# Sixteen of 22 k-pairs in seven products, VectorE's weight sum one quadruple ahead, and a later load for a lone plain quadruple

## The chip, the cores and the metric

The kernel runs on one core of one Trainium2 chip. The metric is the device time of one execution in microseconds (us).

## What is computed

One layer of a hybrid encoder on 256 tokens of width 2048, all in float32. First a mixer (sliding-window attention beside a gated linear recurrence), then the feed-forward block, in which the change lies:

```python
u = h @ w_up                      # 2048 -> 2 * 5632
u = causal depthwise conv of 3 taps(u)
a, b = split(u)
x = x + (silu(a) * b) @ w_down    # 5632 -> 2048
```

## The kernel before, in words

**Products in three parts.** TensorE takes each float32 product as three matmuls: high part by high part, high by low, low by high. A weight block comes from HBM by a DMA that SyncE's queue (SP) issues; ScalarE (ACT) writes its rounded high part (hi); VectorE (DVE) writes the rest, weight minus high part, as its low part (lo); then TensorE may use it. The text calls three such matmuls of 128x128 by 128x512 a **set**.

**The last product**, gated activations by w_down, is the down stage. Its 44 row tiles of w_down make 22 k-pairs. It runs twice, for two pairs of 512 output columns (pair 0 and pair 1), so there are 44 **quadruples** (four 128x512 blocks of w_down and four token-by-column outputs), numbered q = 22 * pair + place here. A quadruple is done in one of two ways. A plain one ("four", lines around 2190) takes 8 sets: two pieces a and b, 4 sets each. A **seven** (function `seven`) is Winograd's form of the 2x2 block product: 7 sets in pieces a (2 sets), b (3) and c (2), with sums of weights and sums of activations. PATTERNS (line 82) writes the kind of each place: S is a seven; C, D, c and d are plain ones. C and D differ in which blocks of the high-part buffer they use; c and d lie in a large slot.

**Where the sums come from.** Two of a seven's weight blocks are sums of neighbours that GpSimd (POOL) forms ahead of time in HBM (u_sums, function `column_block` and the loop behind it): per k-pair two copying DMAs of 512 KB and two accumulating ones, paced by TensorE's progress in steps of SUM_STEP units. The other two sums are VectorE's: t2 = t1 + b21 (line 1694) and t4 = t2 + b22 (line 1696), which fill piece c. They read piece b as loaded. The sums of activations are made by VectorE and ScalarE in the up stage (`sums_of_activations`, `hi_of_sums`), one group each, for the first SEVENS groups; 14 of them stay in SBUF (RESIDENT_SUMS), the others are parked in DRAM (`park_sums`) and fetched back by `fetch_sums` into memory that the x2 tile later takes over. `fetch_x2` brings back the residual in four parts, at the places in X2_BACK_AT.

**Buffers.** From q = 4 on, raw weights and their low parts have three large slots (`slots`), which sevens and c take in turn, and a small one (slot3a, slot3b) for C and D. High parts have two slots, by q modulo 2. So the load of a seven's piece a is issued when the same piece of the seven three turns earlier has been used (`wait_for_slot`, through units_used), and ScalarE's high part of a piece waits until the piece of q - 2 in the same blocks has been used (`hi_piece_before`).

**Order of the work.** Each engine's order is written out. SP: for each q, `load_seven` (four DMAs: line 638, 256 KB, and 639, 256 KB of u_sums, for piece a; line 641, 512 KB, and 643, 256 KB of u_sums, for piece b) or `load_four` (line 650, two DMAs of 512 KB). ScalarE: `hi_of`, the pieces in turn (line 1131); piece c waits for t4. VectorE: `lo_of` (line 1703), which for a seven is: low part of a, t2, t4, low part of b, low part of c (line 1680). At q = 22 and 43 VectorE also merges the Winograd sums of a pair into the output (`free_the_banks`, `rest_of_merge`, `add_last`). TensorE waits with units_split for a piece's low part.

```python
PATTERNS = ["CCCCSSSSSDSSSSSDSSSSSc", "CcSSDSSSSSDSSSSSDSSSCc"]
SUM_STEP = (13, 3)
X2_BACK_AT = [[5, 5, 17, 17], [13, 13, 19, 19]]
```

Of the kernel before, what the change touches and what calls it, by code (L numbers as in the profile page):

```python
# [35 lines left out]
ALU = mybir.AluOpType  # L36
# [42 lines left out]
Q_DOWN = Q_UP + 2 * UP_GROUPS  # L79
QUADRUPLES = KT_FF // 2  # L80
COLUMN_PAIRS = OUT_GROUPS // 2
PATTERNS = ["CCCCSSSSSDSSSSSDSSSSSc", "CcSSDSSSSSDSSSSSDSSSCc"]
KINDS = "".join(PATTERNS)
SEVENS = PATTERNS[0].count("S")
SEVEN_AT = [[at for at, kind in enumerate(pattern) if kind == "S"] for pattern in PATTERNS]
EIGHT_AT = [[at for at, kind in enumerate(pattern) if kind != "S"] for pattern in PATTERNS]
RESIDENT_SUMS = 14
# [8 lines left out]
OLD_RING = 4  # L96
SLOTS = 4
SMALL_SLOT = SLOTS - 1


def slots_in_turn():

    slot_of, turn = [None] * OLD_RING, 0
    for kind in KINDS[OLD_RING:]:
        if kind in "CD":
            slot_of.append(SMALL_SLOT)
        else:
            slot_of.append(turn % SMALL_SLOT)
            turn += 1
    return slot_of  # L110


SLOT_OF = slots_in_turn()
HI_SLOTS = 2
SUM_STEP = (13, 3)
SCRATCH = 1024

G_OUT = 0
# [10 lines left out]
def hybrid_layer(nc, x, attn_norm, w_in, q_norm, k_norm, sinks, lb_logits, hg_norm, w_out,  # L129
                 ffn_norm, w_up, conv_w, conv_b, w_down, out):  # L130
    ctx = ExitStack()
    with ctx:
# [3 lines left out]
        def sem(name):  # L136
            return ctx.enter_context(nc.semaphore(name))
# [223 lines left out]
        down_loaded = {piece: [sem(f"down_loaded_{piece}{n}") for n in range(SLOTS)] for piece in "ab"}  # L361
        four_loaded = {piece: [sem(f"four_loaded_{piece}{n}") for n in range(SMALL_SLOT)] for piece in "ab"}
        t2_made, t4_made = sem("t2_made"), sem("t4_made")
# [52 lines left out]
        def q_of(pair, at):  # L416
            return pair * QUADRUPLES + at

        def is_seven(pair, at):
            return PATTERNS[pair][at] == "S"  # L420

        def seven_of(pair, at):

            return pair * SEVENS + SEVEN_AT[pair].index(at)

        def pieces_of(q):
            return "abc" if is_seven(*divmod(q, QUADRUPLES)) else "ab"

        def piece_number(q, piece):

            return Q_DOWN * RING + sum(len(pieces_of(n)) for n in range(q)) + "abc".index(piece)
# [11 lines left out]
        def raw_piece_before(q, piece):  # L443
            return last_piece_in(q, piece, lambda m: SLOT_OF[m] == SLOT_OF[q], raw_blocks_of)
# [14 lines left out]
        def raw_blocks_of(q, piece):  # L459

            if SLOT_OF[q] == SMALL_SLOT:
                return {"a": slice(0, 2), "b": slice(2, 4)}[piece]
            return blocks_of(q, piece)

        def slot_of(q, piece, as_lo):

            if SLOT_OF[q] == SMALL_SLOT:
                return slot3["ab".index(piece)][as_lo][:, :, :]
            return slots[SLOT_OF[q]][as_lo][:, blocks_of(q, piece), :]

        def raw_of(q, piece):
            return slot_of(q, piece, 0)

        def lo_slot(q, piece):
            return slot_of(q, piece, 1)

        def hi_slot(q, piece):
            return hi_slots[q % HI_SLOTS][:, blocks_of(q, piece), :]
# [4 lines left out]
        def loaded_of(q, piece):  # L483
            return (four_loaded if in_large_slot(q) else down_loaded)[piece][SLOT_OF[q]]

        def down_loads(q):

            n = sum(is_seven(*divmod(m, QUADRUPLES)) + 1 for m in range(OLD_RING, q + 1)
                    if SLOT_OF[m] == SLOT_OF[q] and in_large_slot(m) == in_large_slot(q))
            return 16 * n  # L490

        def wait_for_down(engine, q, piece):
            engine.wait_ge(loaded_of(q, piece), down_loads(q))

        def wait_until_used(engine, number):
            engine.wait_ge(units_used, number + 1 + RING)
# [22 lines left out]
        def out_both(pair):  # L519
            return slice(2 * pair * GT, 2 * (pair + 1) * GT)  # L520
# [1 line left out]
        X2_PARTS = [(1, 1), (1, 0), (0, 0), (0, 1)]  # L522
        X2_PARTS_APART = 2 - (PARKED_SUMS - 1)
        SUMS_BACK_AT = [5, 7]
        X2_BACK_AT = [[5, 5, 17, 17], [13, 13, 19, 19]]
        FIRST_HALF, SECOND_HALF = slice(0, GT // 2), slice(GT // 2, GT)

        def last_half(pair):
# [14 lines left out]
        def _(sp):  # L543
# [16 lines left out]
            for i in range(2):  # L560
                c = slice(i * HEAD_DIM, (i + 1) * HEAD_DIM)
# [44 lines left out]
            def fetch_x2(pair, part):  # L606

                if part == 0 and pair == 0:
                    sp.wait_ge(x2_parked, 16 * OUT_GROUPS)
                t, b = X2_PARTS[part]  # L610
                if part == X2_PARTS_APART:
                    wait_until_used(sp, piece_number(q_of(pair, SEVEN_AT[pair][LAST_PARKED_TURN]), "c"))
                sp.dma_start(x2[:, t, b * GT:(b + 1) * GT], parked_v[:, t, out_columns(pair, b)]).then_inc(x2_back, 16)
# [9 lines left out]
            def wait_for_slot(q, piece):  # L623

                before = raw_piece_before(q, piece)
                if before is not None:
                    wait_until_used(sp, before)
                elif SLOT_OF[q] == 2:
                    wait_until_used(sp, LAST_OLD - 3 if piece == "a" else LAST_OLD - 1)
                elif SLOT_OF[q] == SMALL_SLOT and piece == "b":  # L630
                    wait_until_used(sp, LAST_OLD)
# [13 lines left out]
            def load_four(pair, at):  # L645

                q = q_of(pair, at)
                for r, piece in enumerate("ab"):
                    wait_for_slot(q, piece)
                    sp.dma_start(raw_of(q, piece).rearrange("p b m -> p (b m)"),  # L650
                                 w_down_v[:, 2 * K_PAIR_AT[pair][at] + r, out_both(pair)])\
                        .then_inc(loaded_of(q, piece), 16)
# [5 lines left out]
            for pair in range(COLUMN_PAIRS):  # L658
                for at in range(QUADRUPLES):
# [8 lines left out]
                    for part in range(len(X2_PARTS)):  # L668
                        if at == X2_BACK_AT[pair][part]:
                            fetch_x2(pair, part)  # L670
# [3 lines left out]
        def _(pool):  # L674
# [52 lines left out]
            def wait_for_step(step):  # L727
                pool.wait_ge(units_used, (Q_F0 + 3) * RING + step * SUM_STEP[0] // SUM_STEP[1] + RING)

# [428 lines left out]
        def _(dve):  # L1158
# [63 lines left out]
            for b in (2, 3):  # L1222
                last = dve.memset(bank[b][:, KEYS:], 0.0)
# [3 lines left out]
            for h in range(2):  # L1227
                s = slice(h * HEAD_DIM, (h + 1) * HEAD_DIM)
# [448 lines left out]
            def split(q, piece):  # L1677

                dve.wait_ge(units_hi, piece_number(q, piece) + 1)
                dve.tensor_tensor(lo_slot(q, piece), raw_of(q, piece), hi_slot(q, piece).bitcast(F32),  # L1680
                                  ALU.subtract).then_inc(units_split, 1)

            def sums_of_weights(pair, at):

                q, s = q_of(pair, at), seven_of(pair, at)
                b21, b22, t1 = [raw_of(q, "b")[:, m, :] for m in range(3)]
                t2, t4 = [raw_of(q, "c")[:, m, :] for m in range(2)]
                wait_for_down(dve, q, "b")
                before = raw_piece_before(q, "c")
                if before is not None:  # L1690
                    wait_until_used(dve, before)
                elif SLOT_OF[q] == 2:
                    wait_until_used(dve, LAST_OLD)
                dve.tensor_tensor(t2, t1, b21, ALU.add).then_inc(t2_made, 1)
                dve.wait_ge(t2_made, s + 1)
                dve.tensor_tensor(t4, t2, b22, ALU.add).then_inc(t4_made, 1)  # L1696

            def lo_of(pair, at):

                q = q_of(pair, at)  # L1700
                for piece in pieces_of(q):
                    if piece == "b" and is_seven(pair, at):
                        sums_of_weights(pair, at)
                        dve.wait_ge(t4_made, seven_of(pair, at) + 1)
                    split(q, piece)
                    if (q, piece) == ADDED_BEHIND:
                        add_last(0)
                    if (q, piece) in MERGE_BEHIND:
                        free_the_banks(MERGE_BEHIND.index((q, piece)))
# [12 lines left out]
            for pair in range(COLUMN_PAIRS):  # L1722
                for at in range(QUADRUPLES):
                    if q_of(pair, at) >= OLD_RING:
                        lo_of(pair, at)
                    for merging in range(COLUMN_PAIRS):
                        if q_of(pair, at) == MERGE_BEHIND[merging][0]:
                            rest_of_merge(merging)
# [541 lines left out]
```

## Time and profile before

| what | us |
|---|---|
| median of 3 runs (1083.17 to 1083.44) | 1083.18 |
| the profiled execution | 1083.67 |
| its span in the trace | 1081.9 |
| TensorE busy | 1076.5 (100% of the span) |
| VectorE busy | 908.9 (84%) |
| ScalarE busy | 631.5 (58%) |
| down stage on TensorE, first weight load to last matmul | 859.02 to 1078.34 |

The profiled execution took 1.8 us more than its span, which counts from the first to the last recorded instruction. The granted TensorE clock is full in all slices.

### The profile page before, as it was taken

The numbers are of one execution on the slowest core, as the hardware profiler recorded it, in microseconds if no ns is written. First come the engines' busy times: TensorE is split into PE (matmuls) and PEld (weight loads), VectorE is DVE, ScalarE is ACT, GpSimd is POOL, SyncE is SP. The second block draws the span as 40 slices with busy tenths as digits, with TensorE's granted clock in tenths as the row PEclk, the third lists the DMA queues.
The fourth block names the chain that finished last, engine by engine and source line by source line (L and its number), as shares of the span: only waits on it lengthen the run. The fifth ranks groups of instructions, "written<-read, shape, count | busy, mean of one in ns | idle before, by whom it ended". The sixth has DMA issues, their size and how long they took to land.

```text
span 1081.9 us, 18172 instructions
## 1 busy us (share of the span) xinstructions
PE 1076.5 (100%) x6549; PEld 930.6 (86%) x6549; DVE 908.9 (84%) x1371; ACT 631.5 (58%) x925; POOL 72.0 (7%) x100
## 2 busy tenths in 40 slices
PE   9999999999999999999999999999999999999998
PEld 8888888888888888888888888888898888888887
DVE  6877988889656578888888888887877899999997
ACT  6677666757544655545555555545555566656663
POOL 4500000000000000000000000000000000000000
PEclk9999999999999999999999999999999999999999
DMA  7645677777788968788787878888887877887782
GB/s 262 195 139 154 194 203 228 193 243 203 225 234 259 258 216 245 222 237 218 247 228 233 237 208 256 229 232 239 245 233 223 236 260 263 282 279 254 287 313 95
DMA packets 185070, 249.08 MB, mean 230 GB/s; under 512 B 9125, under 2 KB 143158, under 8 KB 184758
## 3 DMA queue, kind: packets, MB, share of 16 engines
q1 hardware_dynamic: 170118, 212.30, 60.6%
q0 software_dynamic: 12480, 31.46, 15.2%
q10 hardware_dynamic: 2416, 4.60, 1.2%
q8 instruction: 31, 0.51, 0.2%
q14 instruction: 25, 0.20, 0.1%
HBM read 243.75 MB, written 36.04 MB: 259 GB/s over the span
## 4 chain that ended last, share of the span: by engine, by line
PE 98%; DMA 1%; DVE 1%; ACT 0%; issue 0%; SPq 0%; DVEq 0%; ACTq 0%
PE bank L1769 38%; PE bank L1777 20%; PE bank L2154 7%; PE bank L2153 7%; PE bank L2152 7%; PE bank L2005 3%; PE bank L1837 3%; PE bank L1839 3%; PE bank L1838 3%; PE bank L2006 3%; PE bank L2007 3%; PE bank L1739 1%; DMA xt<-in_x_dram 1%; PE bank L2044 0%; PE bank L1924 0%; PE bank L1814 0%
## 5 line engine op out<-in xcount | busy, mean ns | idle before, releaser
L758 ACT CAST w_hi<-raw 128x1024 fp32r<-128x1024 f32 x299 | 313.1, 1051 | 254.8 <-PE bank L1777 122.7
L1161 DVE TENSOR_TENSOR w_lo<-raw,w_hi 128x1024 fp32r<-128x1024 f32 x299 | 363.9, 1222 | 107.7 <-ACT w_hi L758 107.2
L1769 PE MATMUL bank<-hs,w_hi 128*128 128x512 f32 x1792 | 423.0, 391 | 0.0
L1769 PEld LDWEIGHTS bank<-hs,w_hi 128*128 128x128 f32 x1792 | 331.2, 188 | 66.3 <-issue 0.9
L1777 PEld LDWEIGHTS bank<-hs,w_lo 128*128 128x128 f32 x1792 | 224.6, 191 | 5.7 <-issue 0.2
L1777 PE MATMUL bank<-hs,w_lo 128*128 128x256 f32 x1792 | 227.3, 283 | 0.0
L1131 ACT CAST hi_slot<-slot 128x1024 fp32r<-128x1024 f32 (+1 forms) x96 | 110.9, 1188 | 68.5 <-DVE slot L1696 37.3
L1680 DVE TENSOR_TENSOR slot_lo<-slot,hi_slot 128x1024 fp32r<-128x1024 f32 (+1 forms) x96 | 128.7, 1387 | 4.5 <-ACT hi_slot L1131 3.6
L2154 PE MATMUL bank<-hi_slot,gated 128*128 128x512 f32 (+1 forms) x202 | 78.2, 387 | 0.0
L2152 PE MATMUL bank<-hi_slot,gated 128*128 128x512 f32 (+1 forms) x202 | 78.2, 387 | 0.0
L1598 DVE SCALAR_TENSOR_TENSOR C<-U,cols,C 128x256 f32<-128x256 f32 x176 | 73.4, 479 | 0.0
L2153 PE MATMUL bank<-slot_lo,gated 128*128 128x512 f32 (+1 forms) x146 | 56.4, 386 | 0.0
L1062 ACT ACTIVATE C<-U,cols 128x256 f32<-128x256 f32 x88 | 48.2, 596 | 12.1 <-DVE U L1172 12.1
L743 POOL DMA_DIRECT2D u_sums<-in_w_ffn_down_dram x30 | 27.4, 914 | 344.6 <-PE bank L1769 143.7
L1837 PE MATMUL bank<-w_hi,mix 128*128 128x512 f32 x128 | 50.3, 393 | 0.0
L2005 PE MATMUL bank<-w_hi,hs 128*128 128x512 f32 x128 | 50.3, 393 | 0.0
L1839 PE MATMUL bank<-w_hi,mix 128*128 128x512 f32 x128 | 49.9, 390 | 0.0
L2007 PE MATMUL bank<-w_hi,hs 128*128 128x512 f32 x128 | 49.8, 389 | 0.0
L1838 PE MATMUL bank<-w_lo,mix 128*128 128x512 f32 x128 | 49.8, 389 | 0.0
L2006 PE MATMUL bank<-w_lo,hs 128*128 128x512 f32 x128 | 49.8, 389 | 0.0
L2152 PEld LDWEIGHTS bank<-hi_slot,gated 128*128 128x128 f32 x202 | 37.9, 188 | 7.8
L2154 PEld LDWEIGHTS bank<-hi_slot,gated 128*128 128x128 f32 x202 | 37.9, 188 | 7.6
(249 smaller groups left out, 1197.8 us busy)
## 6 DMA issues: line engine op xcount, KB each, us to landing
raw<-in_w_ffn_up_dram SPq DMA_DIRECT2D x176, 512.0 KB, 4.8
u_sums<-in_w_ffn_down_dram POOLq DMA_DIRECT2D x60, 512.0 KB, 6.7
raw<-in_w_in_dram SPq DMA_DIRECT2D x52, 512.0 KB, 4.6
slot<-in_w_ffn_down_dram SPq DMA_DIRECT2D x36, 512.0 KB, 4.8
raw<-in_w_in_dram SPq DMA_DIRECT2D x64, 256.0 KB, 3.3
raw<-in_w_out_dram SPq DMA_DIRECT2D x32, 512.0 KB, 5.1
slot<-u_sums SPq DMA_DIRECT2D x60, 256.0 KB, 5.6
slot<-in_w_ffn_down_dram SPq DMA_DIRECT2D x30, 256.0 KB, 4.1
```

Of the source, the lines that this page charges most:

```text
L758: act.copy(w_hi[:, i, :], raw[:, i, :]).then_inc(units_hi, 1)
L1131: act.copy(hi_slot(q, piece), raw_of(q, piece)).then_inc(units_hi, 1)
L1161: dve.tensor_tensor(w_lo[:, i, :], raw[:, i, :], w_hi[:, i, :].bitcast(F32), ALU.subtract)\
L1680: dve.tensor_tensor(lo_slot(q, piece), raw_of(q, piece), hi_slot(q, piece).bitcast(F32), ALU.subtract).then_inc(units_split, 1)
L1769: m = pe.matmul(banks[b][:, :], w_hi[:, i, c], hs[:, 4 * i + k, :], start=(first and k == 0), stop=(final and k == 3))
L1777: m = pe.matmul(banks[b][:, 0:SEQ], w_lo[:, i, c], hs[:, 4 * i + k, 0:SEQ], start=False, stop=False)
L1837: pe.matmul(banks[t][:, :], x_hi, hi, start=(k0 + k == 0), stop=False)
L1839: last = pe.matmul(banks[t][:, :], x_lo, hi, start=False, stop=(k0 + k == k_all - 1))
L2005: pe.matmul(o, x_hi, hi, start=(u == 0 and k == 0), stop=False)
L2152: pe.matmul(dst[:, :], x_hi, hi, start=start, stop=False)
L2153: pe.matmul(dst[:, :], x_hi, lo, start=False, stop=False)
L2154: return pe.matmul(dst[:, :], x_lo, hi, start=False, stop=stop)
```

## The change

The patterns get one more S per pair (16 instead of 15) and one plain quadruple fewer: q = 9 becomes a seven, D stands at q = 11 alone in pair 0, and nine sevens follow each other from 12 to 20; in pair 1, D stands at 26, 34 and 42, with seven sevens between (27 to 33, 35 to 41). With that SEVENS is 16 and two sums of activations are parked instead of one. POOL's steps are 4 units apart instead of 13/3. The load of every quadruple in the small slot waits until piece b of the quadruple before it has landed. VectorE forms t2 of q + 1 in front of the last low part of q, and t4 behind it, for all sevens from q = 9 on. Three of the four parts of x2 come back at 14 and 15.

```diff
--- before.py
+++ after.py
@@ -79,7 +79,7 @@
 Q_DOWN = Q_UP + 2 * UP_GROUPS
 QUADRUPLES = KT_FF // 2
 COLUMN_PAIRS = OUT_GROUPS // 2
-PATTERNS = ["CCCCSSSSSDSSSSSDSSSSSc", "CcSSDSSSSSDSSSSSDSSSCc"]
+PATTERNS = ["CCCCSSSSSSSDSSSSSSSSSc", "CcSSDSSSSSSSDSSSSSSSDc"]
 KINDS = "".join(PATTERNS)
 SEVENS = PATTERNS[0].count("S")
 SEVEN_AT = [[at for at, kind in enumerate(pattern) if kind == "S"] for pattern in PATTERNS]
@@ -96,6 +96,7 @@
 OLD_RING = 4
 SLOTS = 4
 SMALL_SLOT = SLOTS - 1
+SUMMED_AHEAD = [q for q, kind in enumerate(KINDS) if kind == "S" and q > OLD_RING + 4]
 
 
 def slots_in_turn():
@@ -112,7 +113,7 @@
 
 SLOT_OF = slots_in_turn()
 HI_SLOTS = 2
-SUM_STEP = (13, 3)
+SUM_STEP = (4, 1)
 SCRATCH = 1024
 
 G_OUT = 0
@@ -522,7 +523,7 @@
         X2_PARTS = [(1, 1), (1, 0), (0, 0), (0, 1)]
         X2_PARTS_APART = 2 - (PARKED_SUMS - 1)
         SUMS_BACK_AT = [5, 7]
-        X2_BACK_AT = [[5, 5, 17, 17], [13, 13, 19, 19]]
+        X2_BACK_AT = [[5, 14, 14, 14], [7, 15, 15, 15]]
         FIRST_HALF, SECOND_HALF = slice(0, GT // 2), slice(GT // 2, GT)
 
         def last_half(pair):
@@ -645,6 +646,8 @@
             def load_four(pair, at):
 
                 q = q_of(pair, at)
+                if SLOT_OF[q] == SMALL_SLOT:
+                    wait_for_down(sp, q - 1, "b")
                 for r, piece in enumerate("ab"):
                     wait_for_slot(q, piece)
                     sp.dma_start(raw_of(q, piece).rearrange("p b m -> p (b m)"),
@@ -1680,29 +1683,38 @@
                 dve.tensor_tensor(lo_slot(q, piece), raw_of(q, piece), hi_slot(q, piece).bitcast(F32),
                                   ALU.subtract).then_inc(units_split, 1)
 
-            def sums_of_weights(pair, at):
-
-                q, s = q_of(pair, at), seven_of(pair, at)
-                b21, b22, t1 = [raw_of(q, "b")[:, m, :] for m in range(3)]
-                t2, t4 = [raw_of(q, "c")[:, m, :] for m in range(2)]
+            def first_sum_of_weights(q):
+
+                b21, _, t1 = [raw_of(q, "b")[:, m, :] for m in range(3)]
                 wait_for_down(dve, q, "b")
                 before = raw_piece_before(q, "c")
                 if before is not None:
                     wait_until_used(dve, before)
                 elif SLOT_OF[q] == 2:
                     wait_until_used(dve, LAST_OLD)
-                dve.tensor_tensor(t2, t1, b21, ALU.add).then_inc(t2_made, 1)
-                dve.wait_ge(t2_made, s + 1)
-                dve.tensor_tensor(t4, t2, b22, ALU.add).then_inc(t4_made, 1)
-
-            def lo_of(pair, at):
-
-                q = q_of(pair, at)
+                dve.tensor_tensor(raw_of(q, "c")[:, 0, :], t1, b21, ALU.add).then_inc(t2_made, 1)
+
+            def second_sum_of_weights(q):
+
+                t2, t4 = [raw_of(q, "c")[:, m, :] for m in range(2)]
+                dve.wait_ge(t2_made, seven_of(*divmod(q, QUADRUPLES)) + 1)
+                dve.tensor_tensor(t4, t2, raw_of(q, "b")[:, 1, :], ALU.add).then_inc(t4_made, 1)
+
+            def lo_of(q):
+
+                here, after = KINDS[q] == "S", q + 1 in SUMMED_AHEAD
                 for piece in pieces_of(q):
-                    if piece == "b" and is_seven(pair, at):
-                        sums_of_weights(pair, at)
-                        dve.wait_ge(t4_made, seven_of(pair, at) + 1)
+                    last = piece == pieces_of(q)[-1]
+                    if last and after:
+                        first_sum_of_weights(q + 1)
+                    if here and piece == "b":
+                        if q not in SUMMED_AHEAD:
+                            first_sum_of_weights(q)
+                            second_sum_of_weights(q)
+                        dve.wait_ge(t4_made, seven_of(*divmod(q, QUADRUPLES)) + 1)
                     split(q, piece)
+                    if last and after:
+                        second_sum_of_weights(q + 1)
                     if (q, piece) == ADDED_BEHIND:
                         add_last(0)
                     if (q, piece) in MERGE_BEHIND:
@@ -1722,7 +1734,7 @@
             for pair in range(COLUMN_PAIRS):
                 for at in range(QUADRUPLES):
                     if q_of(pair, at) >= OLD_RING:
-                        lo_of(pair, at)
+                        lo_of(q_of(pair, at))
                     for merging in range(COLUMN_PAIRS):
                         if q_of(pair, at) == MERGE_BEHIND[merging][0]:
                             rest_of_merge(merging)
```

## Rows read from the trace of the kernel before

**Rows 1.** The page's chain that ended last, by engine.
```profile
PE 98%; DMA 1%; DVE 1%; ACT 0%; issue 0%; SPq 0%; DVEq 0%; ACTq 0%
```

**Rows 2.** Whom TensorE waited for: total us, times, longest; the longest wait.
```profile
PE bank L1744 <- DVE all_mean L1221: 1.1, 1, 1.1
```

**Rows 3.** Busy time by stretch: PE, PEld, DVE, ACT, POOL, clock, DMA share, GB/s.
```profile
1009.00:1019.00 10.00, 10.00 (x46) 8.29 (x45) 9.91 (x10) 6.89 (x6) 0.00 (x0) 1.00 0.99 354
760.00:859.00 99.00, 99.00 (x573) 87.75 (x572) 78.64 (x107) 50.84 (x63) 6.01 (x8) 1.00 0.83 234
```

**Rows 4.** TensorE's timeline, start and duration: two weight loads, the last matmul.
```profile
859.02 0.19 PEld L2152 LDWEIGHTS bank<-w_hi,gated 128*128 128x128 f32 x1
...
859.70 0.19 PEld L2152 LDWEIGHTS bank<-w_hi,gated 128*128 128x128 f32 x1
...
1078.34 0.28 PE L2154 MATMUL bank<-hi_slot,gated 128*128 128x256 f32 x1
```

**Rows 5.** VectorE's timeline around the plain quadruple 9 and the seven 10.
```profile
897.64 2.90 DVE L1680 TENSOR_TENSOR slot_lo<-slot,hi_slot 128x1536 fp32r<-128x1536 f32 x2
900.45 1.22 DVE L1680 TENSOR_TENSOR slot3a_lo<-slot3a,hi_slot 128x1024 fp32r<-128x1024 f32 x1
...
902.75 1.22 DVE L1680 TENSOR_TENSOR slot_lo<-slot,hi_slot 128x1024 fp32r<-128x1024 f32 x1
903.89 0.69 DVE L1694 TENSOR_TENSOR slot<-slot 128x512 f32<-128x512 f32 x1
904.61 0.69 DVE L1696 TENSOR_TENSOR slot<-slot 128x512 f32<-128x512 f32 x1
905.34 4.03 DVE L1680 TENSOR_TENSOR slot_lo<-slot,hi_slot 128x1536 fp32r<-128x1536 f32 x3
909.28 0.68 DVE L1694 TENSOR_TENSOR slot<-slot 128x512 f32<-128x512 f32 x1
```

**Rows 6.** VectorE's timeline in the merge of q = 22.
```profile
963.58 0.69 DVE L1662 TENSOR_TENSOR x<-x,bank 128x512 f32<-128x512 f32 x1
964.18 0.68 DVE L1663 TENSOR_TENSOR x<-x,bank 128x512 f32<-128x512 f32 x1
...
966.70 1.22 DVE L1680 TENSOR_TENSOR slot3b_lo<-slot3b,hi_slot 128x1024 fp32r<-128x1024 f32 x1
```

**Rows 7.** SyncE's queue: issue time and duration of DMAs.
```profile
899.25 0.43 SPq L643 DMA_DIRECT2D slot<-u_sums  x1
...
911.80 0.33 SPq L638 DMA_DIRECT2D slot<-in_w_ffn_down_dram  x1
...
919.44 0.43 SPq L650 DMA_DIRECT2D slot3a<-in_w_ffn_down_dram  x1
...
953.96 0.33 SPq L650 DMA_DIRECT2D slot<-in_w_ffn_down_dram  x1
```

**Rows 8.** DMAs issued at 899.25, 911.80, 953.96, 954.33, 955.32, 1035.34: size, us to landing.
```profile
slot<-u_sums SPq DMA_DIRECT2D x1, 256.0 KB, 5.3
slot<-in_w_ffn_down_dram SPq DMA_DIRECT2D x1, 256.0 KB, 3.3
slot<-in_w_ffn_down_dram SPq DMA_DIRECT2D x1, 512.0 KB, 4.7
slot3a<-in_w_ffn_down_dram SPq DMA_DIRECT2D x1, 512.0 KB, 6.4
slot<-in_w_ffn_down_dram SPq DMA_DIRECT2D x1, 512.0 KB, 8.8
slot<-u_sums SPq DMA_DIRECT2D x1, 256.0 KB, 9.1
```

**Rows 9.** VectorE's timeline at the seven 14, behind whose load stood a plain one.
```profile
926.44 0.69 DVE L1694 TENSOR_TENSOR slot<-slot 128x512 f32<-128x512 f32 x1 [0.89 <-DMA slot<-u_sums]
...
928.02 1.76 DVE L1680 TENSOR_TENSOR slot_lo<-slot,hi_slot 128x1536 fp32r<-128x1536 f32 x1 [0.17 <-ACT hi_slot L1131]
```

**Rows 10.** The DMA view of 900 to 960: GB/s in 40 slices of 1.5 us.
```profile
GB/s 376 380 332 229 315 130 0 0 67 229 217 307 220 307 325 335 195 365 417 391 381 376 404 376 391 117 11 0 168 209 287 302 232 280 333 232 107 257 393 243
```

**Rows 11.** The up stage, 400 to 859: one of VectorE's sums of activations.
```profile
L1635 DVE TENSOR_TENSOR C<-C 128x128 f32<-128x128 f32 x15 | 4.4, 292 | 0.5
```

## The prediction

> **What bounds the kernel now.** I read the chain of waits first: TensorE holds 98% of it [rows 1]. The waits by engine come next: the longest wait of TensorE in the whole execution is 1.1 us, at its start [rows 2]. So the kernel is as long as TensorE's instructions, and whatever shortens them helps until another engine falls behind. The busy time by stretch shows which one is near: in the down stage VectorE is busy 9.91 of 10 us, in the up stage 78.6 of 99 [rows 3]. The timelines then give each price.
>
> TensorE: a set takes 859.70 - 859.02 = 0.68 us [rows 4]. Counting from 859.02, 320 full sets of 0.680 and the last four of half width (0.36 each) end at 1078.2, and the last matmul starts at 1078.34 [rows 4]: no stall in the stage. A seven is 7 x 0.68 = 4.76 us, a plain quadruple 8 x 0.68 = 5.44.
>
> VectorE: from t2 of one seven to t2 of the next is 909.28 - 903.89 = 5.39 us, of which t2 and t4 are 905.34 - 903.89 = 1.45 and the three low parts 3.94 [rows 5]. A plain quadruple is 902.75 - 900.45 = 2.30. So VectorE loses 0.63 us on each seven and gains 3.14 on each plain one. It lives on its lead, which the plain quadruples refill. At q = 14 its low part of b ends at 928.02 + 1.76 = 929.78 [rows 9]; TensorE comes there 105 sets after 859.02, at 930.46. That lead is 0.7 us.
>
> **The change, part by part.**
>
> *One more seven per pair.* Two sets less: -1.36 us of TensorE, on the path. VectorE gets a seven for a plain one, twice.
>
> *t2 ahead.* t4 needs t2, so today it starts 0.72 behind it [rows 5]. Two sums that don't need each other start 0.60 apart [rows 6]. With a low part between them I price each at 0.60: a seven is 3.94 + 1.20 = 5.14 us, and its loss is 0.38. This holds for the 27 sevens from q = 9 on: 27 x 0.25 = 6.8 us less. Two exchanged quadruples add 2 x (5.14 - 2.30) = 5.7. In sum VectorE has 1.1 us less to do and TensorE 1.36 less, so the balance of the stage is as before. What counts is the order. The Trainium skill ("VectorE: DVE Perf Modes", "The DRAIN you can't avoid") says that chained operations take the same time with or without a semaphore between them; by it the new order saves nothing and a seven stays at 5.39. The rows speak against it: 0.72 with the wait, 0.60 without.
>
> *The new run 4 to 10.* VectorE is at the low part of c of q = 8 at 897.64 + 1.67 = 899.31 [rows 5]. Now t2 of 9 stands ahead of it. The b of 10 is loaded at 899.25 + 5.3 = 904.55 [rows 7, 8]; that of 9 is one seven earlier, at 899.8. From there, with 0.60 for a sum, 1.14 and 1.67 for low parts: t2 899.8, c 900.4, t4 901.5, a 902.1, b 903.3; then t2 of 10 904.95, c 905.55, t4 906.7, a 907.3, b 908.4 to 910.2, c to 911.3. TensorE needs b of 10 at 910.7 and c at 912.8. The thinnest lead is 0.5. No stall, taken at 0; half a microsecond more lateness would show.
>
> *The later load.* TensorE reaches q = 11 (D) at 859.02 + 81 x 0.68 = 914.13 and q = 12 at 919.57. SP now waits for b of 10, until 904.6. D's two loads follow at 904.6 and 905.1, and right behind them, since their slot has been free from 903.2 (65 sets), those of q = 12: 905.6, 906.0, 906.4, 906.8. The last one brings the sum block that t2 of 12 needs. So 2.36 MB are asked for within 2.2 us, and q = 13 adds its own from 907.2. D itself lands in time: the first two of such a burst took 4.7 and 6.4 us [rows 8], 909.3 to 911.5, and TensorE wants it at 914.1.
>
> When does b of 12 land? Call it x. The nearest case is the burst at 953.96, four loads of 512 KB (2.10 MB) in 1.4 us: the last landed at 955.32 + 8.8 = 964.1, 10.15 behind the first issue [rows 7, 8]. From 904.65 that gives 914.8; the 0.26 MB more, at the 354 GB/s of [rows 3], give 915.5. I take the middle, x = 915.2. Lower end: the fastest first landing, 3.3 [rows 8], and 2.1 MB behind it at 417 GB/s, the best slice of [rows 10], give 912.9. Upper end: 906.85 + 9.1, the slowest landing of such a block [rows 8], 916.0.
>
> What x costs: VectorE does t2 at x, low b of 11 (ends x + 1.82), t4, a of 12, b of 12 (ends x + 5.23). With 0.1 for the signal, TensorE waits at b of 11 (due 916.85) from x = 914.9 on, and comes to b of 12 with a lead of 915.6 - x, or 0.7 once it has itself waited. Eight sevens follow in pair 0, 8 x 0.38 = 3.0 us of loss: the stall is x - 912.6. In pair 1, D at 34 meets the same order with six sevens behind b of 35, 2.3 us of loss: the stall is the same x less 913.3 (in pair 0's time). At 915.2 that is 2.6 + 1.9 = 4.5; at the ends 0.3 and 6.1. At q = 26 the wait costs nothing, since the small slot is still in use then. At q = 22 it puts the loads some 4 us later, behind which come the merge and its 12 sums; the lead there was 971.3 (165 sets) less 966.70 + 1.22 [rows 6], 3.4 us, and TensorE is late by then itself: 0, at most 1.5.
>
> *The rest, at zero.* Four more GpSimd DMAs before the down stage (64 for 60) in 252 units instead of 256, off every chain; the last is issued earlier than now. Six more operations of VectorE on one up group, about 2 us at 0.29 and more apiece [rows 11], beside 20 idle of 99 [rows 3]; ScalarE's two copies and the second parked block likewise. Fetching 0.39 MB more of parked sums lies at q = 5 and 29, and the three x2 parts at 14 and 15, where nothing is due for some 8 us. Without these covers they would cost up to 1 us each.
>
> **Sum.** -1.36 + 4.5 = +3.1. The profiled execution took 1083.67 (its span and 1.8 around it), 0.5 above the median of the runs; it would become 1086.8. Against the median of 1083.18 that is **1086.3 us**.
>
> **The rivals.**
> *In time after all (not slower).* If the burst is moved at the lower end's rate, x is 912.9, the lead of 2.7 at b of 12 lasts over nearly all nine sevens, and the result is 1083.18 - 1.36 + 0.3 = 1082.1. It decides at the landing of b of 12: each 0.1 us earlier than 915.2 gives back 0.2. For it: the total of bytes is small against 10 us, and D's load no longer stands beside b of 10, the thing that made VectorE wait 0.89 us at q = 14 [rows 9]. Against it: the burst at 953.96. [...]
> *Half.* x between 913.5 and 914.7: stalls of 1 to 3.5 us, about 1083.5.
> *The new order saves nothing.* A seven stays at 5.39: losses of 0.63 over eight and six sevens, 4.4 and 3.1, and 1.3 more at q = 9, 10, 27 to 33 and 11: 1083.18 - 1.36 + 8.8 = 1090.6.
> *The merge at q = 22 is late too:* 1.5 more, 1087.7.
> *Something not seen* makes it faster by more than 1.36 us, which the products removed can't.
>
> **How the numbers follow.** About 0.2% (2.2 us) is what a measurement of this kernel can tell from no change. Forecast 0.47; in time 0.26; half 0.16; merge late too 0.05; order saves nothing 0.04; not seen 0.02. Slower: 0.47 + 0.05 + 0.04 = 0.56. Same: 0.26 + 0.16 = 0.42, since 1082.1 is only 0.1% below. Faster: 0.02. The range holds in time, half and the forecast with its upper end (1083.18 - 1.36 + 6.1 = 1087.9): 1081.8 to 1088.0. The forecast's own is 1085.4 to 1088.0.
>
> **What would show it.** TensorE's waits must show low parts of pieces (line 1680) for q = 11 or 12, 16 to 20 and 38 to 41, in all 4 to 5 us; VectorE idle some 3 us ahead of t2 of 12 and of 35, released by a DMA of u_sums; those blocks landing 8 us or more behind their issue. A seven on VectorE at 5.14 us shows the order right. If TensorE has no wait in the stage and the last matmul starts 1.4 us earlier, the late load was wrong; a pitch of 5.39 means the order was.

## The result, and the profile after

The changed kernel takes **1085.65 us** (median of 13 runs, 1085.0 to 1086.63), the kernel before beside it 1083.09 (13 runs, 1082.94 to 1083.44). The ratio is 1.0023, with a 95% interval of 1.0016 to 1.0031: slower by 2.6 us. Predicted were 1086.3 and a range of 1081.8 to 1088.0. The profiled execution took 1085.14, its span 1083.4.

The chain of waits is TensorE's as before [rows 1], and TensorE's longest wait is still the 1.1 us at its start [rows 2]:

```profile
PE 99%; DVE 1%; ACT 0%; issue 0%; DVEq 0%; ACTq 0%
```

The down stage tells the difference. TensorE's timeline, with its first and last weight load of the stage (the last of before stood at 1078.22):

```profile
858.25 0.19 PEld L2164 LDWEIGHTS bank<-w_hi,gated 128*128 128x128 f32 x1
...
1079.73 0.19 PEld L2166 LDWEIGHTS bank<-hi_slot,gated 128*128 128x128 f32 x1
```

From first to last that is 221.48 us; before, 1078.22 - 859.02 = 219.20, without a stall. Two sets fewer would make it 217.84. So **the stage has 3.64 us of stalls** and is 2.28 longer. Below, the stall of any kernel with 16 sevens is its length less 217.84, and of one with 15 less 219.20. (That the stage starts 0.77 us earlier comes from the start-up and not from the change: six small weight loads there took 0.74 us in this profile and 1.34 in that of before, and in a run below whose kernel differs from before only by SyncE's wait in the down stage they took 0.74 too, and the stage starts at 858.43.)

The waits by engine between 859 and 1082 name who holds TensorE up (columns: total us, times, longest):

```profile
ACT hi_slot L1134 <- DVE slot L1701: 40.1, 27, 2.0
...
DVE slot L1695 <- DMA slot<-u_sums: 7.0, 4, 2.3
PEld bank L2164 <- DVE slot_lo L1683: 6.3, 21, 0.4
...
DVE slot_lo L1683 <- ACT hi_slot L1134: 0.7, 2, 0.4
```

TensorE waits 21 times for a low part. The 6.3 us are more than the stall of 3.64, because each wait as shown has some 0.13 us in it that TensorE doesn't lose: a small gap stands ahead of any weight load, and the load behind a wait follows sooner than usual. VectorE, in turn, waited four times for the block that its sum t2 reads, 7.0 us in all. ScalarE's 40 us are its waits for t4, and they reach nobody: VectorE waited for a high part of a seven only 0.7 us. VectorE's timeline has the four, and between them seven after seven without a gap:

```profile
899.23 0.69 DVE L1695 TENSOR_TENSOR slot<-slot 128x512 f32<-128x512 f32 x1 [1.06 <-DMA slot<-u_sums]
...
913.51 0.69 DVE L1695 TENSOR_TENSOR slot<-slot 128x512 f32<-128x512 f32 x1 [1.62 <-DMA slot<-u_sums]
...
918.66 0.69 DVE L1695 TENSOR_TENSOR slot<-slot 128x512 f32<-128x512 f32 x1
919.26 1.22 DVE L1683 TENSOR_TENSOR slot_lo<-slot,hi_slot 128x1024 fp32r<-128x1024 f32 x1
920.39 0.69 DVE L1701 TENSOR_TENSOR slot<-slot 128x512 f32<-128x512 f32 x1
921.00 2.89 DVE L1683 TENSOR_TENSOR slot_lo<-slot,hi_slot 128x1024 fp32r<-128x1024 f32 x2
923.80 0.69 DVE L1695 TENSOR_TENSOR slot<-slot 128x512 f32<-128x512 f32 x1
...
1004.31 0.69 DVE L1695 TENSOR_TENSOR slot<-slot 128x512 f32<-128x512 f32 x1 [2.30 <-DMA slot<-u_sums]
...
1029.27 0.69 DVE L1695 TENSOR_TENSOR slot<-slot 128x512 f32<-128x512 f32 x1 [2.02 <-DMA slot<-u_sums]
```

The idle times belong to t2 of q = 9, 12, 30 and 35. From 918.66 to 923.80 is 5.14 us, a seven in the new order (5.39 in the old [rows 5]).

SyncE's queue shows the burst that the new wait makes: D's two loads, then the four of q = 12. The landings under it are those of the loads issued at 903.69, 904.06 and 906.29:

```profile
903.69 0.33 SPq L653 DMA_DIRECT2D slot3a<-in_w_ffn_down_dram  x1
904.06 0.43 SPq L653 DMA_DIRECT2D slot3b<-in_w_ffn_down_dram  x1
904.54 0.43 SPq L639 DMA_DIRECT2D slot<-in_w_ffn_down_dram  x1
905.01 0.52 SPq L640 DMA_DIRECT2D slot<-u_sums  x1
905.58 0.67 SPq L642 DMA_DIRECT2D slot<-in_w_ffn_down_dram  x1
906.29 0.65 SPq L644 DMA_DIRECT2D slot<-u_sums  x1
```

```profile
slot3a<-in_w_ffn_down_dram SPq DMA_DIRECT2D x1, 512.0 KB, 4.1
...
slot3b<-in_w_ffn_down_dram SPq DMA_DIRECT2D x1, 512.0 KB, 6.2
...
slot<-u_sums SPq DMA_DIRECT2D x1, 256.0 KB, 7.2
```

906.29 + 7.2 = 913.5, which is where t2 of 12 starts. The busy time by stretch (columns as in [rows 3]) shows it from the other side: around the burst VectorE is not full and the DMAs move 402 GB/s; in the stalls at 939 it is full to the last hundredth; 1019 holds the wait for b of 35.

```profile
909.00:919.00 10.00, 10.00 (x46) 8.27 (x45) 8.38 (x9) 6.62 (x6) 0.00 (x0) 1.00 1.04 402
939.00:949.00 10.00, 9.99 (x43) 7.51 (x42) 10.00 (x11) 6.47 (x7) 0.00 (x0) 1.00 0.77 267
...
1019.00:1029.00 10.00, 9.98 (x44) 7.69 (x43) 8.25 (x8) 5.51 (x6) 0.00 (x0) 1.00 0.86 263
```

Note that a stalled TensorE still reads 9.99 of 10 busy; only the starts of its weight loads, and their number (x42 against x45), tell.

**Two theories.** The wait at q = 30 (1004.31) is the longest of the four, and no load of a plain quadruple is near it: the last block of b of 30 was issued at 998.79 and landed 5.5 us later, which is what such a block takes in a steady run (5.3 in [rows 8]). The prediction has no such wait. So there are two explanations to weigh:

- *A, the burst*: SyncE's wait bunches D's loads with the next seven's, so b of 12 and b of 35 are late.
- *B, the cap*: t2 of q + 1 now stands in front of q's last low part, so b of q + 1 is wanted some 2.0 us earlier than in the old order: 5.14 us ahead of the end of its low part, where it was 1.45 + 1.67 = 3.12. But its load can't be issued earlier: it waits until b of three turns before has been used. Once VectorE has a good lead, it runs into that landing and idles; the lead is cut, at q = 30 to about 0.75 us: low b of 30 ends at 1009.46, and TensorE comes to it 221 sets and 1.7 us of stall behind 858.25, at 1010.2.

### The profile page after: what moved, and what is told of

It is laid out like the page before. It is cut to its first block, busy times and chain, and to the rows that moved or that the text cites. A ratio compares the mean times of both kernels' runs of the same rounds, so it can differ in the third digit from the quotient of the medians.

```text
span 1083.4 us, 18159 instructions
## 1 busy us (share of the span) xinstructions
PE 1078.1 (100%) x6543; PEld 927.1 (86%) x6543; DVE 911.1 (84%) x1383; ACT 632.5 (58%) x929; POOL 75.1 (7%) x104
## 4 chain that ended last, share of the span: by engine, by line
PE 99%; DVE 1%; ACT 0%; issue 0%; DVEq 0%; ACTq 0%
PE bank L1781 38%; PE bank L1789 20%; PE bank L2164 7%; PE bank L2165 7%; PE bank L2166 7%; PE bank L2017 3%; PE bank L1849 3%; PE bank L2019 3%; PE bank L1850 3%; PE bank L1851 3%; PE bank L2018 3%; PE bank L1751 1%; PE bank L1756 1%; PE bank L2056 0%; PE bank L1936 0%; PE bank L1826 0%
## 5 line engine op out<-in xcount | busy, mean ns | idle before, releaser
L1134 ACT CAST hi_slot<-slot 128x1024 fp32r<-128x1024 f32 (+1 forms) x102 | 116.4, 1186 | 67.1 <-DVE slot L1701 40.1
L1683 DVE TENSOR_TENSOR slot_lo<-slot,hi_slot 128x1024 fp32r<-128x1024 f32 (+1 forms) x102 | 138.1, 1387 | 0.9 <-ACT hi_slot L1134 0.7
L2164 PE MATMUL bank<-hi_slot,gated 128*128 128x512 f32 (+1 forms) x194 | 75.5, 389 | 0.0
L2166 PE MATMUL bank<-hi_slot,gated 128*128 128x512 f32 (+1 forms) x194 | 75.1, 387 | 0.0
L2165 PE MATMUL bank<-slot_lo,gated 128*128 128x512 f32 (+1 forms) x154 | 59.6, 387 | 0.0
L2164 PEld LDWEIGHTS bank<-hi_slot,gated 128*128 128x128 f32 x194 | 36.4, 188 | 9.1 <-DVE slot_lo L1683 1.7
L2166 PEld LDWEIGHTS bank<-hi_slot,gated 128*128 128x128 f32 x194 | 36.4, 188 | 7.6
```

The lines of the kernel that those rows point to most:

```text
L1134: act.copy(hi_slot(q, piece), raw_of(q, piece)).then_inc(units_hi, 1)
L2164: pe.matmul(dst[:, :], x_hi, hi, start=start, stop=False)
L2165: pe.matmul(dst[:, :], x_hi, lo, start=False, stop=False)
L2166: return pe.matmul(dst[:, :], x_lo, hi, start=False, stop=stop)
```

## The experiments

"Stall" is as defined above, from the profiled execution. Ratios are against the kernel before, timed beside each run.

### One part of the change undone: the late load

The wait is taken out; everything else is as after.

```diff
-                if SLOT_OF[q] == SMALL_SLOT:
-                    wait_for_down(sp, q - 1, "b")
```

> The changed kernel without SyncE's wait ahead of the small slot's loads. Theory A (the burst: the wait makes D's loads and those of the next seven one burst, and b of 12 and of 35 land late): most of the 3.7 us of TensorE's waits goes, about 1 us is left, 1083.0 us, and VectorE's idle time ahead of t2 of 12 and 35 falls from 1.6 and 2.0 us to under 0.8. Theory B (the cap: with t2 formed one piece earlier, a load that is issued when b of the seven three turns before is used comes too late for any lead over 0.7 us, whoever waits in SyncE): 2.2 to 3.2 us of waits stay, in the last sevens of each run, 1083.9 to 1084.9 us.

Measured: 1084.37 us (11 runs, 1083.49 to 1084.76), ratio 1.0009 (1.0000 to 1.0019); stage 220.64, stall 2.80. This is theory B's range; A's 1083.0 is out. The wait is worth 0.8 us by the stage and 1.3 by the medians, no more. VectorE's timeline shows what is left (its waits of over 1 us):

```profile
906.02 0.69 DVE L1693 TENSOR_TENSOR slot<-slot 128x512 f32<-128x512 f32 x1 [1.34 <-DMA slot<-u_sums]
...
1005.06 0.69 DVE L1693 TENSOR_TENSOR slot<-slot 128x512 f32<-128x512 f32 x1 [2.57 <-DMA slot<-u_sums]
```

The second is the wait at q = 30 again, without any burst. The first is t2 of 10: D's loads are back beside b of 10. The wait had moved that lateness from 10 to 12, not only made one. So 1.1 of the 2.8 us, at q = 9 and 10, come from D's loads together with the early t2, and 1.7 from the last sevens of the runs.

### One part undone: the sum's place

```diff
-SUMMED_AHEAD = [q for q, kind in enumerate(KINDS) if kind == "S" and q > OLD_RING + 4]
+SUMMED_AHEAD = []
```

> The changed kernel with both weight sums behind the seven's own piece a, as before (a seven takes VectorE 5.39 us instead of 5.14). Theory A: the late burst stays and each seven loses 0.63 instead of 0.38: the waits grow to 5 to 6 us, 1087.0 us. Theory B: the cap on the lead rises from 0.7 to 2.7 us and pays for the slower sevens: 2 to 3 us of waits, 1083.7 to 1084.7 us.

Measured: 1087.23 us (5 runs, 1085.52 to 1087.46), ratio 1.0035 (1.0021 to 1.0049); stage 223.06, stall 5.22. Here A is right and B wrong: with 16 sevens and the late load, the old order is 1.6 us worse, not better. TensorE's weight loads show why: the same load of each seven starts 5.39 us behind that of the last, which is VectorE's pitch and not TensorE's 4.76, so every seven loses its whole deficit of 0.63 (the wait shown, 0.72, has in it the small gap that stands ahead of any weight load):

```profile
945.46 0.19 PEld L2164 LDWEIGHTS bank<-hi_slot,s_hi 128*128 128x128 f32 x1 [0.72 <-DVE slot_lo L1683]
950.86 0.19 PEld L2164 LDWEIGHTS bank<-hi_slot,s_hi 128*128 128x128 f32 x1 [0.72 <-DVE slot_lo L1683]
956.25 0.19 PEld L2164 LDWEIGHTS bank<-hi_slot,s_hi 128*128 128x128 f32 x1 [0.72 <-DVE slot_lo L1683]
961.64 0.19 PEld L2164 LDWEIGHTS bank<-hi_slot,s_hi_top 128*128 128x128 f32 x1 [0.74 <-DVE slot_lo L1683]
```

So the sum ahead has two effects: it saves 0.25 us a seven, which pays in long runs, and it caps the lead, which costs where the lead would have been larger. A had the saving and B the cap; neither had both. No run here has sixteen sevens, the old order throughout and no late load, so what the old order would cost there by itself is not shown.

### One part alone: the sum ahead, on the kernel before

The before kernel's patterns, step and places of x2, no late load, with t2 ahead from q = 10 on.

```diff
+SUMMED_AHEAD = [q for q, kind in enumerate(KINDS) if kind == "S" and q > OLD_RING + 4]
```

> The kernel before with the new order of VectorE's sums alone (fifteen sevens). Both theories: no change of time beyond 0.2 us, 1083.1 us, since runs of five sevens never used up the lead. A: VectorE gets ahead and waits for its inputs more. B shows in the trace: t2 of the fourth and fifth seven of each run waits for a DMA of u_sums by up to 2 us, and TensorE comes within 0.3 to 0.7 us of waiting there.

Measured: 1083.80 us (11 runs, 1083.26 to 1084.31), ratio 1.0007 (0.9998 to 1.0016); stage 219.86, stall 0.66, all of it at 1042 and 1044. VectorE has some 6 us less to do (25 sevens at 0.25) and TensorE the same, yet a stage that had no stall has one. The timeline shows where VectorE's saving went, two of eight waits:

```profile
918.78 0.69 DVE L1693 TENSOR_TENSOR slot<-slot 128x512 f32<-128x512 f32 x1 [2.25 <-DMA slot<-u_sums]
...
1002.73 0.69 DVE L1693 TENSOR_TENSOR slot<-slot 128x512 f32<-128x512 f32 x1 [1.79 <-DMA slot<-u_sums]
```

The waits are B's, of the fourth seven of a run, and of the size that it gave them. Both theories had the time within 0.2 us, though; the median is 0.7 us above before's, with an interval that only just includes no change.

### One part alone: the late load, on the kernel before

```diff
                 q = q_of(pair, at)
+                if SLOT_OF[q] == SMALL_SLOT:
+                    wait_for_down(sp, q - 1, "b")
```

> The kernel before with SyncE's wait alone. Theory A: the b of the sevens behind a D (10, 16, 33, 39) lands 8 to 9 us behind its issue, and the longest runs (five sevens) lose up to 1 us each: 1083.1 to 1085 us. Theory B: the wait by itself costs nothing, 1083.1 us within 0.2.

Measured: 1083.34 us (11 runs, 1083.04 to 1083.66), ratio 1.0002 (0.9993 to 1.0011); stage 219.2, no stall. The burst is there: the loads of the plain quadruple at 15 went out at 923.90 and 924.28 (919.44 and 919.92 before), and those of q = 16 from 924.75 on, right behind them. It costs nothing that can be seen here. Two things differ from the kernel after, VectorE wants b later and five sevens follow, not nine, and no run tells which of them counts.

### The sum ahead only where its load has time or the lead is small

t2 stands ahead for 15 sevens: q = 5, the first two or three behind each plain quadruple, and three more in the middle of pair 0's nine (18 to 20). First without the late load, then with it.

```diff
+SUMMED_AHEAD = [5, 12, 13, 14, 18, 19, 20, 24, 25, 27, 28, 29, 35, 36, 37]
```

> The changed kernel without SyncE's wait, and with t2 ahead only for the sevens 5, 12 to 14, 18 to 20, 24, 25, 27 to 29 and 35 to 37: where the load has a plain quadruple's time to spare, or where the lead is under 0.7 us anyhow. Theory B (the order ahead caps the lead at 0.7 us in a steady run, the old order at 2.7): the lead lasts, TensorE waits 0 to 0.8 us in all, 1081.7 to 1082.6 us. Theory A alone (only the burst and the 0.25 us per seven count): ten sevens lose 0.25 us each more than without the wait, 1085 us or more.

Measured: 1082.70 us (11 runs, 1081.89 to 1083.25), ratio 0.9995 (0.9986 to 1.0004); stage 219.09, stall 1.25, all between 948 and 960, behind one wait of VectorE, 1.02 us ahead of t2 of 18. A's 1085 is out; B's ranges (a stall up to 0.8, 1082.6 us) are passed by 0.45 and 0.1, because the lead was not small at q = 18, where t2 stands ahead again.

> As e5_chosen_ahead, with SyncE's wait kept. The wait puts b of 12 and 35 at 7 to 8 us behind their issue and their issue 2.5 us later, so the lead at 12 and 35 is 1 to 1.5 us instead of 3.6, and the sevens behind them use it up: TensorE waits 3.5 to 5 us, 1085.3 to 1086.8 us. If the wait is harmless by itself, the time is that of e5_chosen_ahead within 0.5 us.

Measured: 1087.96 us (5 runs, 1087.7 to 1089.21), ratio 1.0045 (1.0031 to 1.0059); stage 224.79, stall 6.95. **The wait that cost 0.8 to 1.3 us in the order of after costs 5.3 here**, more than either theory gave it. VectorE's timeline and TensorE's weight loads show the same burst, worse placed:

```profile
915.79 0.69 DVE L1695 TENSOR_TENSOR slot<-slot 128x512 f32<-128x512 f32 x1 [3.86 <-DMA slot<-u_sums]
```

```profile
917.67 0.19 PEld L2164 LDWEIGHTS bank<-hi_slot,gated 128*128 128x128 f32 x1 [1.00 <-DVE slot3b_lo L1683]
```

D's loads went out 904.83 - 858.91 = 45.9 us behind the stage's start, 0.5 later than in the kernel after (903.69 - 858.25 = 45.4). The last block of q = 12 was issued at 907.36, and t2 of 12 starts 8.4 behind that. t2 of 12 stands in front of the low part of b of 11, and TensorE waited a whole microsecond for that one: the wait that the prediction named for q = 11, and that the kernel after does not have. From there on every seven in the old order pays its full deficit.

### D's loads one at a time, and early

The set of the 15 sevens again, no late load; the loads of D at q = 11, 34 and 42 are issued apart, piece a behind the loads of q - 2 and piece b behind those of q - 1.

```diff
+            SPLIT_EARLY = [11, 34, 42]
...
+                    for q, piece in ((q_of(pair, at) + 2, "a"), (q_of(pair, at) + 1, "b")):
+                        if q in SPLIT_EARLY:
+                            load_piece(q, piece)
```

> As e5_chosen_ahead, and the loads of D at 11, 34 and 42 issued one by one: piece a behind the loads of the seven two before, piece b behind those of the seven one before. The same bytes, no 1 MB block: b of 10 and 33 should land 6 to 7 us behind their issue instead of 7.4, b of 12 and 35 about 6. If bursts still cost anything there, 0.3 to 0.8 us less than e5_chosen_ahead; if its lead covers them, the same time within 0.3 us.

Measured: 1082.32 us (11 runs, 1081.77 to 1083.01), ratio 0.9992 (0.9983 to 1.0001); stage 219.07, stall 1.23. Against the run with D's loads together the stage is the same, and 0.4 us of the medians is within what executions differ by. It has the lowest median of all.

> The changed kernel (t2 ahead for all) with the loads of D at 11, 34 and 42 split as in e7_chosen_ahead_split and no wait. Theory A: spreading the loads is what the wait tried; under 1 us of TensorE's waits, 1082.5 us. Theory B: the cap in the last sevens of each run stays, 1.2 us in pair 0, 0.4 in 27 to 33, 0.5 in 35 to 41, and about 0.5 from D beside b of 10: 2.0 to 2.8 us, 1083.8 to 1084.6 us.

This one has the early, split loads with every t2 ahead, as after. Measured: 1084.67 us (11 runs, 1083.98 to 1086.17), ratio 1.0015 (1.0006 to 1.0024); stage 221.07, stall 3.23. That is a little above B's ranges, and far from A's 1082.5. With D's loads spread the stall is 3.2 of after's 3.6. **The larger part of the loss comes from where the sums stand ahead**, not from the late load: between this kernel and the one above only the set differs, and it is worth 2.0 us of stage and 2.35 of time.

The 3.2 us are not the cap alone. D's piece a was issued at 894.32, right behind the last block of b of 9 (893.84), and that block took 6.7 us where it took 5.5 in the first experiment. The early t2 of 9 waits for it, the longest wait of VectorE in this run:

```profile
900.58 0.69 DVE L1706 TENSOR_TENSOR slot<-slot 128x512 f32<-128x512 f32 x1 [2.20 <-DMA slot<-u_sums]
```

By its weight loads TensorE lost 0.8 us at q = 9 and 10, then 1.2 in the last four sevens of pair 0 and 1.2 in pair 1. With the chosen set the same loads cost it nothing at q = 9 and 10 and nothing in pair 1; the 1.2 in pair 0 are there too, behind t2 of 18.

### Where in a run the sum may stand ahead

Split loads, no late load; the set is cut to the sevens that follow a plain quadruple (first diff), or has 15 to 17 in place of 12 to 14 (second). VectorE's work is the same in both.

```diff
+SUMMED_AHEAD = [5, 12, 13, 14, 24, 25, 27, 28, 29, 35, 36, 37]
```

> As e7_chosen_ahead_split, but with the sevens 18 to 20 in the old order: t2 ahead for 5, 12 to 14, 24, 25, 27 to 29, 35 to 37 only. In e7_chosen_ahead_split VectorE idled 1.29 us ahead of t2 of 18 and TensorE then waited 1.2 us in all. Theory B (the order ahead throws away any lead over 0.7 us in a steady run): VectorE comes to 18 with 2.3 us of lead, loses 0.63 on each of three, and TensorE waits nowhere: 1081.7 us. If only VectorE's work counts, three sevens at 0.25 us more each make it slower than e7_chosen_ahead_split by 0.5 to 0.8 us, 1083.0 us.

Measured: 1082.69 us (11 runs, 1082.37 to 1084.33), ratio 0.9998 (0.9989 to 1.0007); stage 218.64, the shortest of all, stall 0.80. VectorE doesn't wait once for a load ahead of t2, although it has three sums fewer ahead. Behind a plain quadruple the load has time: the last block of b of 12 was issued at 903.38, landed 6.1 us later, and t2 of 12 starts at 911.34, with low b of 12 done 3.8 us before TensorE comes to it. All that is left of TensorE's waits:

```profile
PEld bank L2175 <- DVE slot_lo L1694: 1.0, 2, 0.7
...
PE bank L2175 <- DVE slot_lo L1694: 0.3, 1, 0.3
```

The expectation was no stall and 1081.7 us; the nine sevens of pair 0 still run out of lead at the last two. The median is 0.37 above that of the kernel with 18 to 20 ahead as well, though its stage is 0.43 shorter; which of the two is faster stays open, since their intervals overlap for the most part, and the start of the stage alone varies by up to 0.8 us between the profiles (858.2 to 859.0).

```diff
+SUMMED_AHEAD = [5, 15, 16, 17, 24, 25, 27, 28, 29, 35, 36, 37]
```

> As e9_ahead_behind_plain, with t2 ahead for 15 to 17 in place of 12 to 14: VectorE's work is the same, only the place differs. If only the work counts: the same time. Theory B: at 15 the lead is cut from 2.3 to 0.7 us (VectorE idle some 1.5 us ahead of t2 of 15, released by a DMA of u_sums), 0.1 is left at 17, and 18 to 20 lose 0.63 each: TensorE waits about 2 us, all in pair 0, 1083.7 us.

Measured: 1083.63 us (11 runs, 1083.18 to 1084.42), ratio 1.0005 (0.9996 to 1.0014); stage 219.41, stall 1.57. The place does matter: with the same sums ahead, 0.77 us more stall and 0.94 more time. But B's sizes were off: VectorE waited 0.30 us ahead of t2 of 15, not 1.5. So there was less lead to cap at q = 15 than the 2.3 us that I had reckoned; where the rest had gone I didn't measure.

Last, the set behind plain quadruples with D's loads together at their old place:

> As e9_ahead_behind_plain, with D's loads together and at their old place (no split, no wait). If the lead covers D's block: the same time within 0.3 us, TensorE without waits. If D's block beside b of 10 costs: up to 0.8 us more.

Measured: 1082.84 us (11 runs, 1082.58 to 1083.61), ratio 0.9999 (0.9990 to 1.0008); stage 218.91, stall 1.07. The same time within 0.3 us, as expected, but not without waits: they are those of the run with D's loads split, at the last two sevens of pair 0, and longer. Splitting D's loads is worth 0.27 us of stage, a size that the medians can't tell.

No version beats the kernel before by more than its interval. The best would be 0.8 us faster (0.9983 to 1.0001).

## Why the prediction was right, point by point

- **TensorE, -1.36 us.** Held: the stage of 218.64 with 16 sevens has two waits left, 0.31 and 0.70 us. Without them it is 217.6, and with the small gap that each of them has in it about 217.8, against 219.20 - 1.36 = 217.84. (One sum of this part slipped: 320 sets and four of 0.36 behind 859.02 end at 1078.06 and not 1078.2. Nothing hangs on it.)
- **A seven at 5.14 us with t2 ahead.** Held to the hundredth. The Trainium skill ("VectorE: DVE Perf Modes", "The DRAIN you can't avoid") says that a chain of operations takes the same time with or without semaphores between them; by that the prediction had it stay at 5.39 as a rival, at 1090.6 us (the run with the old order took 1087.23). This case's traces speak against taking it so: a sum starts 0.72 behind another whose result it waits for, and an independent operation 0.61 behind the same sum.
- **q = 9 and 10, no stall.** Held. The wait ahead of t2 of 9 was 1.06 us and not 0.5. Low b of 10 ends at 909.5 (t2 of 10 at 904.38 and 5.14), and TensorE comes to it 76 sets behind 858.25, at 909.9: a lead of 0.4 against 0.5.
- **The landing of b of 12, x = 915.2 (912.9 to 916.0).** Measured 913.5, which in before's time, 0.77 us later, is 914.3: it landed 0.9 us earlier than taken, the last block in 7.2 us where the prediction, from the burst at 953.96, had 8.3. D itself took 4.1 and 6.2 us against 4.7 and 6.4.
- **What x costs in pair 0, x - 912.6.** 1.7 for 914.3; measured 1.7 (TensorE started b of 20 at 959.95, and 147 sets behind 858.25 would be 958.2; it makes up 0.1 of it right behind). Its waits stand where they were put, at q = 16 to 20. The one at b of 11 was not there, since x lay below 914.9.
- **Pair 1, x - 913.3.** 1.0 for 914.3; measured 1.6 from q = 34 on, since b of 35 took 8.0 us where b of 12 took 7.2.
- **Not in the sum: the cap.** t2 of 30 waited 2.30 us and the end of that run (b of 32, then a and b of 33) cost TensorE some 0.4. With the lead of 0.75 at q = 30 and 0.38 lost on each of three sevens, 0.39 was to be expected, had the cap been seen. The step that missed it is the one that followed VectorE from 897.64 through q = 10 and then took the rest of each run from the loss of 0.38 alone; it asked whether t2 is in time only beside a late load, never in a steady run. The same step made the late load look like the whole cause. With it away, 2.8 us of stall remained, and with split loads 3.2, of which 1.2 stood in the last sevens of pair 0, where the sum above has only the burst. So the two causes overlap there, and by the sum's rule the kernel without the late load should have come near "in time after all", 1082.1 us; it took 1084.37.
- **q = 22, the merge, at 0.** Held: low part and TensorE's loads there show no wait.
- **The rest at zero** (GpSimd's DMAs, six more sums of activations, parked sums and x2): held as far as can be seen; TensorE waits for nothing else in the stage. No run changes GpSimd's steps or the places of x2 by themselves. The stall and the two sets account for -1.36 + 3.64 = +2.28 of a measured +2.56.

The stalls were forecast as 4.5 us from one cause and came to 3.6 from two. By the terms: x came 0.9 us earlier, in two pairs, -1.8; b of 35 was later than b of 12, +0.6; the cap, +0.4; 4.5 - 1.8 + 0.6 + 0.4 = 3.7. That the forecast of the time was near is in part luck: one term taken too large stood for one that was left out.

## What to carry to other kernels

Before you move an operation ahead of another, ask what its input waits for: an operation that stands one piece earlier wants its input one piece earlier, and if the load's issue is tied to the release of a buffer, the lead of that engine is cut to what the ring allows, even while its busy time falls. Move it only where the input has time to spare, as here behind a plain quadruple, whose load takes a buffer of its own, or where the lead is small anyway. And a wait that holds back one load holds back all that stand behind it in that queue: its price is that of the burst it makes, and here it went from nothing that could be seen to 5.3 us, with the number of sevens behind it and the order of another engine's work.

## What the runs showed of the hardware

- On VectorE a sum of 128x512 started 0.72 us behind another whose result it reads (903.89 and 904.61 [rows 5]), and an independent operation 0.60 to 0.61 behind such a sum (918.66 and 919.26 in the kernel after).
- The last 256 KB of D's burst landed 7.2 us (b of 12) and 8.0 (b of 35) behind their issue in the kernel after and 8.4 in the chosen order with the late load, against 5.2 to 5.5 in a steady run. A load can also delay one that was issued ahead of it: the last block of b of 9 took 6.7 us with 512 KB issued 0.48 behind it, and 5.5 without.
- Loads of one queue don't always land in the order of issue. In the kernel before, 512 KB issued at 1033.58 took 9.3 us and landed at 1042.9; 256 KB issued 1.39 us behind them, at 1034.97, took 7.3 and landed at 1042.3.
- The profile's TensorE column said 9.99 of 10 us busy in a stretch (939 to 949 in the kernel after) with four waits for a low part, 1.1 us in all. The count of weight loads, 42 against 45 in a stretch without a wait, did not hide them.
